# Last residual, final norm and store with tokens on partitions, and two waits taken from the expert passes

## The reference

```python
def _moe(h, w_router, b_router, we1, we3, we2):
    logits = (x @ w_router).astype(f32) + b_router.astype(f32)
    top_v, top_i = lax.top_k(logits, TOP_K)            # 2 of 8 experts for each token
    gates = jax.nn.softmax(top_v, axis=-1)
    comb = jnp.sum(jax.nn.one_hot(top_i, N_EXPERTS, dtype=f32) * gates[..., None], axis=1)
    for e in range(N_EXPERTS):
        y = y + comb[:, e:e + 1] * _swiglu(x, we1[e], we3[e], we2[e]).astype(f32)
...
    x = x + g2 * ffn          # g2: 1024 gates, one row for the prompt, one for each of the 8 sequences
...
    y = _rmsnorm(x, p['final_g'])
```

## Time and profile before

| what | us |
|---|---|
| time, median of 3 runs | 2700.26 |
| lowest and highest of these | 2694.53, 2711.96 |
| time of the profiled execution | 2696.46 |
| its span, first to last instruction | 2694.8 |
| PE busy | 2305.4 (86%) |
| DVE busy | 1541.6 (57%) |
| ACT busy | 1156.8 (43%) |
| POOL busy | 150.9 (6%) |

### The profile page before, as it was taken

One profiled execution on the slowest core, in us unless ns is written; L12 is line 12 of the kernel. 1 busy time (PEld: TensorE's weight loads), 2 busy tenths in 40 slices (PEclk: granted clock), 3 DMA queues, 4 the chain that ended last, 5 costly groups with the idle time before them and its releaser, 6 DMA issues. The chain is left out here.

```text
span 2694.8 us, 37681 instructions
## 1 busy us (share of the span) xinstructions
PE 2305.4 (86%) x14185; PEld 1986.0 (74%) x14185; DVE 1541.6 (57%) x2167; ACT 1156.8 (43%) x1551; POOL 150.9 (6%) x256
## 2 busy tenths in 40 slices
PE   6899985778699999898999768576999999999973
PEld 3799763448699989898997535466878787878762
DVE  0456637323543444444565382437888887888864
ACT  3332114322433333333221144225777777777753
POOL 2000001101000000000000011100000000000001
PEclk6699766858799999997997678687999999999985
DMA  7122415351254454541223235108999999999962
GB/s 237 54 79 63 165 56 174 128 179 56 79 157 132 133 140 133 142 142 32 63 79 102 83 101 194 43 7 313 350 348 364 373 354 351 375 356 358 377 245 86
DMA packets 285562, 485.05 MB, mean 180 GB/s; under 512 B 21614, under 2 KB 216696, under 8 KB 285440
## 3 DMA queue, kind: packets, MB, share of 16 engines
q1 hardware_dynamic: 264816, 416.42, 44.7%
q0 software_dynamic: 20624, 66.91, 7.1%
HBM read 455.79 MB, written 26.97 MB: 179 GB/s over the span
## 5 line engine op out<-in xcount | busy, mean ns | idle before, releaser
L837 PE MATMUL banks<-upper_parts,region_split 128*128 128x320 f32 x1664 | 397.3, 314 | 37.1 <-DVE weights_lower L2081 29.3
L2081 DVE TENSOR_TENSOR expert_lower<-expert_ring,region_split 128x1408 fp32r<-128x1408 f32 (+1 forms) x270 | 387.6, 1467 | 28.1 <-ACT region_split L1567 19.0
L837 PE MATMUL banks<-region_split 128*128 128x320 f32 (+1 forms) x1376 | 378.2, 338 | 28.2 <-DVE region L2081 14.8
L837 PE MATMUL banks<-upper_parts,weights_lower 128*128 128x320 f32 x1248 | 390.1, 313 | 0.0
L1567 ACT ACTIVATE region_split<-expert_ring 128x1408 fp32r<-128x1408 f32 (+1 forms) x270 | 330.5, 1256 | 58.4 <-DMA expert_ring<-in_we 50.5
L837 PEld LDWEIGHTS banks<-upper_parts,region_split 128*128 128x128 f32 x1664 | 290.1, 192 | 38.9 <-DVE weights_lower L2081 35.9
L837 PE MATMUL banks<-region_split,upper_parts 128*128 128x512 f32 (+1 forms) x996 | 300.1, 377 | 1.4 <-DVE upper_parts L2081 1.4
L837 PEld LDWEIGHTS banks<-region_split 128*128 128x128 f32 x1376 | 245.5, 189 | 48.4 <-issue 33.2
L837 PE MATMUL banks<-z_weights_upper,upper_parts 128*128 128x256 f32 (+3 forms) x844 | 262.3, 343 | 14.2 <-DVE region_split L2081 14.2
L837 PE MATMUL banks<-expert_lower,upper_parts 128*128 128x512 f32 x720 | 269.2, 374 | 0.0
L1567 ACT ACTIVATE region_split<-weight_ring 128x2048 fp32r<-128x2048 f32 (+2 forms) x72 | 141.0, 1960 | 253.1 <-PE banks L837 226.0
(11 more groups left out here) (294 smaller groups left out, 3575.3 us busy)
## 6 DMA issues: line engine op xcount, KB each, us to landing
expert_ring<-in_we SPq DMA_DIRECT2D x240, 704.0 KB, 8.0
expert_ring<-in_we SPq DMA_DIRECT2D x165, 512.0 KB, 4.5
weight_ring<-in_w_ada SPq DMA_DIRECT2D x48, 1024.0 KB, 7.4
weight_ring<-in_w SPq DMA_DIRECT2D x88, 512.0 KB, 4.6
weight_ring<-in_w_in SPq DMA_DIRECT2D x24, 1024.0 KB, 5.3
weight_ring<-in_w SPq DMA_DIRECT2D x16, 1408.0 KB, 6.3
weight_ring<-in_w_out SPq DMA_DIRECT2D x8, 1024.0 KB, 8.6
y_rows<-hidden_t POOLq DMA_DIRECT2D x15, 512.0 KB, 7.7
```

Of the source, the lines that this page charges most:

```text
L837: return nc.tensor.matmul(out, lhsT, rhs, start=first, stop=last)
L2081: return v.tensor_tensor(out, x, y, op)
```

## The change

1. **Tail.** `YA` and `YC` have five tiles each, and POOL issues all ten gathers in a row. The rest stays with tokens on partitions: DVE adds the second result, multiplies by the gates and adds the residual, on rows of 1024; ACT squares and sums each row (`accum_out`) and takes the root; DVE takes the reciprocal and multiplies by it and by `final_g`; POOL stores each tile of 512 KB. The transposes, the norm over `XT`, the barriers and the copies into `YO` are gone.
2. **Residual and gate rows.** For that, `XT` is turned block by block in place, and the gates are turned into `GATE_ROWS` (two rows of 1024, for the prompt tiles and for the sample tile, on all partitions). Each is a unit of four 128 x 128 blocks in one bank. Five units of the residual stand in `route1` (`EARLY_ROWS`), five more and four of the gates at the start of `ffn1` (`LATE_ROWS`). `KEPT_BY` says who copies each late unit out. `final_g` is loaded on all partitions into `FINAL_ROW`, an eighth transfer on `router_in`.
3. **Passes.** The wait for `product_made` ahead of `down`, in the loop and behind it, is gone; `turn_product` waits for its own part, and parts 0 and 1 are turned into banks 3 and 4, where before they went into 1 and 2.

```diff
-        YA, YC = r(2, D), r(2, D)
+        YA, YC = r(NT, D), r(NT, D)
...
+        def token_rows(t, half):
+
+            return XT[:, 4 * half:4 * half + 4, tiles(t)]
+
+        EARLY_ROWS = [(t, half) for t in range(NT) for half in range(2)][:5]
+        LATE_ROWS = [(t, half) for t in range(NT) for half in range(2)][5:] + [("gates", i, half) for i in range(2) for half in range(2)]
+        KEPT_BY = ["dve", "dve", "act", "act", "act", "act", "dve", "dve", "dve"]
...
-                         (SNUM[:, :], c["slot_numbers"]), (PFIRST[:, :], c["pass_firsts"]))
+                         (SNUM[:, :], c["slot_numbers"]), (PFIRST[:, :], c["pass_firsts"]),
+                         (FINAL_ROW, a["final_g"].rearrange("(one n) -> one n", one=1).broadcast_to([P, D])))
...
                     for t in range(NT):
-                        if t >= 2:
-                            pool.wait_ge(pair_used, t - 1)
                         for dst, slot in ((YA, SLOT1), (YC, SLOT2)):
                             pool.indirect_dma_start(
-                                dst[:, t % 2, :], None, d["y_rows"],
+                                dst[:, t, :], None, d["y_rows"],
...
             for t in range(NT):
-                for half in range(2):
-                    pool.wait_ge(y_rows_ready, 2 * t + half + 1)
...
+                pool.wait_ge(y_rows_ready, t + 1)
+                load(y_out, (o["y_prompt"][0, tiles(t), :] if t < NTP else o["y_sample"].rearrange("b t d -> (b t) d"), YA[:, t, :]))
...
                     turn_hidden(4)
+                    for u, (t, half) in enumerate(EARLY_ROWS):
+                        b = 4 + (2 * NT + u) % 4
+                        claim(b)
+                        for j in range(4):
+                            ins = tr(PS[:, b, tiles(j)], XT[:, 4 * half + j, tiles(t)])
+                        hand(ins, "act", b)
                     take(one_hots_ready)
...
                         first, end = PARTS[part]
+                        wait(product_made, n.value("product_made") - 2 + part)
                         claim(bank)
...
-                                turn_product(f // 4 - 1, f // 4)
+                                turn_product(f // 4 - 1, 2 + f // 4)
...
+                    for u, unit in enumerate(LATE_ROWS):
+                        b = u % 6
+                        claim(b)
+                        for j in range(4):
+                            if unit[0] == "gates":
...
+                                columns = MOD[:, l, 5 * KD + k, 0:1].broadcast_to([P, P]) if unit[1] == 0 else GATES_SPREAD[:, k, :]
+                                ins = mm(PS[:, b, tiles(j)], columns, ident[:, :], True, True)
+                            else:
+                                ins = tr(PS[:, b, tiles(j)], XT[:, 4 * unit[1] + j, tiles(unit[0])])
+                        holder[b] = hand(ins, KEPT_BY[u], b)
...
-                        wait(product_made, n.value("product_made"))
                         down(True, True)
...
-                    wait(product_made, n.value("product_made"))
                     down(False, True)
...
+                    scale_first(0)
                     for t in range(NT):
+                        if t + 1 < NT:
+                            scale_first(t + 1)
+                        take(tokens_summed)
+                        link(func(YC[:, t, :], YA[:, t, :], ACT.Square, accum_out=SQUARES[:, t:t + 1]))
+                        func(TOKEN_ROOT[:, t:t + 1], SQUARES[:, t:t + 1], ACT.Sqrt, scale=1.0 / D, bias=eps[:, 0:1])\
+                            .then_inc(token_root_ready, 1)
...
+                    copy(GATES_SPREAD.rearrange("p k (b t) -> p k b t", t=TS), along(MOD[:, l, 5 * KD:6 * KD, 1:], 3, TS)).then_inc(gates_spread, 1)
+                    keep(range(2))
                     for _ in range(AHEAD):
                         lower(FE)
+                    keep(range(6, 9))
...
+                    def normalise_rows(t):
+
+                        take(token_root_ready)
+                        link(v.reciprocal(TOKEN_ROOT[:, t:t + 1], TOKEN_ROOT[:, t:t + 1]))
+                        stt(YA[:, t, :], YA[:, t, :], TOKEN_ROOT[:, t:t + 1], FINAL_ROW, ALU.mult, ALU.mult).then_inc(y_rows_ready, 1)
...
+                        link(stt(YA[:, t, :], YC[:, t, :], GB[:, t:t + 1], YA[:, t, :], ALU.mult, ALU.add))
+                        link(tt(YA[:, t, :], YA[:, t, :], GATE_ROWS[:, t // NTP, :], ALU.mult))
+                        by_rows = YA[:, t, :].rearrange("p (k c) -> p k c", c=P)
+                        tt(by_rows, by_rows, XT[:, :, tiles(t)], ALU.add).then_inc(tokens_summed, 1)
+                        if t:
+                            normalise_rows(t - 1)
+                    normalise_rows(NT - 1)
```

More of the change, by code:

```diff
@@ L1322, in _ @@
                 if l % 2:
-                    take(router_in, 112)
+                    take(router_in, 128)
                     claim(0, 1)
@@ L1457, in _ @@
                     for part in range(3):
-                        wait(product_made, n.value("product_made") - 2 + part)
                         turn_product(part, 6 + part % 2)
@@ L1481, in _ @@
                     stage(f"ffn{l}")
-                    for t in range(NT):
-                        take(pair_summed)
-                        for half in range(2):
-                            b = 2 * (t % 2) + half
-                            claim(b)
-                            for k in range(4):
-                                ins = tr(PS[:, b, tiles(k)], YA[:, t % 2, tiles(4 * half + k)])
-                            hand(ins, "dve", b)
-                        pe.drain().then_inc(pair_used, 1)
-                    stage(f"resid{l}")
                     continue
@@ L1543, in _ @@
                 stage(f"ffn{l}")
-                stage(f"resid{l}")
-            norm()
-            stage("norm_final")
-            for t in range(NT):
-                for half in range(2):
-                    b = (2 * t + half) % 8
-                    claim(b)
-                    for k in range(4):
-                        ins = tr(PS[:, b, tiles(k)], HT[:, 4 * half + k, tiles(t)])
-                    hand(ins, "act", b)
-            stage("store")
         @block.scalar
@@ L1903, in _ @@
                     func(E2[:, :], E2[:, :], ACT.Exp).then_inc(pair_exp_ready, 1)
+                    for u, unit in enumerate(EARLY_ROWS):
+                        take(for_act)
+                        drained(copy(kept_rows(unit), PS[:, 4 + (2 * NT + u) % 4, :].rearrange("p (k c) -> p k c", c=P)))
                 stage(f"route{l}")
@@ L1964, in _ @@
                         upper(FE)
+                    for u, unit in enumerate(LATE_ROWS):
+                        if KEPT_BY[u] == "act":
+                            take(for_act)
+                            drained(copy(kept_rows(unit), PS[:, u % 6, :].rearrange("p (k c) -> p k c", c=P)))
                     for half in range(2):
@@ L2033, in _ @@
                 stage(f"ffn{l}")
-                stage(f"resid{l}")
-            root()
-            for k in range(KD):
-                modulate(k, VEC[:, V_FIN + k:V_FIN + k + 1], None)
-            stage("norm_final")
-            for u in range(2 * NT):
-                take(for_act)
-                if u >= 4:
-                    act.wait_ge(y_out[u % 4], 16 * (u // 4))
-                drained(copy(YO[:, u % 4, :], PS[:, u % 8, :]))
-                also(y_rows_ready)
-            stage("store")
         @block.vector
@@ L2771, in _ @@
                 stage(f"ffn{l}")
-                stage(f"resid{l}")
-            norm(along(along(VEC[:, V_FIN:V_FIN + KD], 2, NB), 3, TS), None)
-            stage("norm_final")
-            stage("store")
 _INS = ["x_prompt", "x_sample", "c_prompt", "c_sample", "cache_k", "cache_v", "cache_kidx", "state_C", "state_n",
```

83 lines of the change are left out of this document (34 added, 49 removed).

## The result

| what | before | with the change |
|---|---|---|
| first comparison, median, us | 2706.11 (4 runs) | 2668.09 (4 runs) |
| second comparison, median, us | 2709.97 (11 runs) | 2677.94 (6 runs) |
| profiled execution, us | 2696.46 | 2679.24 |

The ratio is 0.988 (95% interval 0.983 to 0.992) in the first comparison and 0.977 (0.972 to 0.982) in the second. By the medians of all executions the change saves 38 and 32 us, by the means 38 and 39; the forecast was 50. The time of 2668 lies in the range of 2637 to 2671, near its upper end; the 2678 of the second comparison lies above it.

A forecast was written before the change was run, and what follows sets the result against it. PE and transfers both near their limit in the passes, PE setting the pace at the wait; the tail bound by its chain. Gains 32.3 + 14.8 + 3.0 = 50.1 us off 2696.46 gave 2646.4; it said 2648, range 2637 to 2671.

The forecast's parts named there:

- The tail: From first gather to last store: the chain of work tile by tile gets shorter, 32.3 us gained, bounds 29 to 34.5.
- The sum on DVE: In the tail: DVE's operations added up, 3.8 us for a tile's sum and 1.5 for its norm, 5.3 a tile.
- The lead-in: Ahead of the passes: added PE work lies in idle time and later matmuls run faster, 3 us gained for both places.
- The one-hot products: In the lead-in: with PE kept busy ahead of them they may run at 2.4 GHz, 4.46 to 2.4 us.
- The two waits: PE's waits for the product ahead of `down`, in and behind the loop: 14 x 1.06 = 14.8 us gained, bounds 0 to 18.
- At bank 5 it may ... I stay at 14.8: In `up`: the wait on the split product may grow by what was saved; unused transfer time speaks against it, so 14.8 us stays.
- the starving of the earlier trace: Around the wait ahead of `down`: transfers ran at 255 and 183 GB/s, leaving 1.5 us of transfer time unused.
- the 13.1 us: PE's wait on the split product, 11 times in twelve passes, read as `up`'s claim of bank 5 for the third part.
- The first: Rival: the transfers set the pass; PE comes earlier to bank 5 and waits there; 2663 to 2667 us, chance 0.20.
- the transfers' total: In a pass: 18.3 MB at an HBM limit of about 358 GB/s, so the pass couldn't be shorter than it is.
- The rival of the clock: In the passes: a PE without pauses is held back more often, time 2700 or 2717 us; chance 0.02.
- The exchange of banks: In the passes: turning parts 0 and 1 into banks 3 and 4 costs nothing, as DVE reads these long before row 4.

The follow-up runs named there:

- e8: Changed kernel without the multiplication by the gates in the tail; tail 40.0 us, where the change had 45.3.
- e7: Changed kernel without the ten units that turn the residual (four of the gates stay); lead-in 132.23 us, where the change had 128.67.
- e3: Changed kernel with ACT and DVE splitting the turned product ahead of the row of weights behind which it stood; 48.02 us a pass.
- e4: Changed kernel with two matmuls instead of three for each product in the expert passes; 44.70 us a pass.
- e1: Changed kernel with the two waits for the whole product put back ahead of `down`, banks 3 and 4 kept; 50.65 us a pass.
- e2: Changed kernel with product parts 0 and 1 turned into banks 1 and 2 as before, the waits still away; 50.75 us a pass.
- e6: The kernel of e3 with the two waits for the whole product put back ahead of `down`; 49.84 us a pass.
- e11: The kernel of e3, timed against the kernel before; median 2634.69 us, ratio 0.970.
- e12: The changed kernel again, timed beside e11 against the kernel before; median 2677.94 us, ratio 0.977.
- e5: Changed kernel with the `up` rows of weights loaded and split over half their columns, its own order of splits; 47.85 to 47.87 us a pass.

## Why the prediction was right or wrong

- **The tail: right.** 32.3 forecast; 33.5 to 34.0 in the executions with the full tail (45.3 to 45.7 us). The sum on DVE was the right one (e8). A tile took 5.10 us, and not 5.3, since neighbouring operations overlap a little.
- **The lead-in: right.** 3.0 forecast; 3.2 measured, 3.4 in the mean of eleven. The one-hot products went from 4.46 to 2.4 as worked out (in the first changed trace only to 3.94), and e7 shows that it hangs on the added rows.
- **The two waits: wrong.** The step that failed is "At bank 5 it may ... I stay at 14.8": I took the starving of the earlier trace rows as proof that the weights, and with them everything at bank 5, would move along with PE. What moves bank 5's end is ACT's and DVE's order: the last splits of the product stand behind rows of weights that arrive at the transfers' full rate. That chain didn't start earlier: the splits end 0.83 us later behind the turns. The reading of the earlier trace rows was wrong as well: the 13.1 us are waits at bank 2, for part 1, so two parts stood in the way and not one. Without a dip a pass gained 50.53 - 50.21 = 0.3 us instead of 1.06, and the dips took that back: 14.8 forecast, 4 in the first pair of traces, about nothing over the 48 passes (50.81 against 50.75).
- **The rivals.** The first had the place right ("PE comes earlier to bank 5 and waits there"), its time was the nearest (2663 to 2667, chance 0.20), and its sign nearly came: a pass still at 50.5 with 2.2 us at bank 5 was named, and it was 50.41 with 1.74 at banks 4 and 5 together. Its mechanism, the transfers' total, is refuted by e3 and e4. That 2668 lies inside the range owes nothing to the two waits. The rival of the clock had a real effect and the wrong cause: I had a PE without pauses held back, but it was held back behind pauses, at 1.7 us a dip.
- **The exchange of banks** was put at nothing, and no run shows it to cost more. It moved part 1's wait from bank 2 to bank 4. With it and the two waits (e1) a pass took 50.65 us against 50.75 before; without it (e2) 50.75 against 50.81 of the changed code.

The sum after the runs: tail 33.8, lead-in 3.4, twelve passes 0.7 lost, the stretch behind them 1.3 lost in the mean of its four executions, so 35 us, between the 38 and 32 of the two comparisons. That the 14.8 were there to be had is shown by e6 against e3: with the product split first, the two waits are worth 1.8 us a pass, 25.5 us over the twelve passes and the stretch behind them (688.03 against 662.55), of which 6.7 are longer busy time of PE.

What stays open is why e6's wait for the product is 1.06 in some passes and 2.0 in others, and why passes with the same idle time at the banks dip in some cases (28) and not in others (34).

## What to carry to other kernels

When a wait is taken away, follow the engine to its next wait and ask what sets the end of that one. If it is another engine working through a fixed order, the saved time arrives there as longer waiting, unless that order changes too. A low rate of the transfers at the wait says that they could do more, not that the work behind them will come earlier: here a short urgent split (0.5 us) stood behind a long one (1.4 us) that could wait, and exchanging the two gave 2.8 us a pass, 43 in the timed medians (e11 against e12), where removing the wait gave none. And pauses of PE can cost more than their length, when its clock falls behind them.

## What the runs showed of the hardware

The clock fell behind pauses of 1.6 us and more in 28 passes of 62 that had them, and not at all in the 36 of e3, e5 and e11, with 0.6 us at most at a time, so a full PE was the faster and the steadier one (47.86 or 47.87 us in nearly all passes of these three).

POOL's copy of one column, 0.18 us before and in e1 and e6, took 1.05 in the twelve passes of the changed kernel, and up to 1.95 in e3. DVE and POOL in the change, then in e3:

```profile
2089.95 2.35 DVE L2081 TENSOR_TENSOR expert_lower<-expert_ring,region_split 128x1024 fp32r<-128x1024 f32 x2
2091.30 1.05 POOL L768 COPY pass_tokens<-token_table 128x1 int32 x1 [29.97 <-PE banks L848]
```

```profile
2067.74 2.35 DVE L2081 TENSOR_TENSOR expert_lower<-expert_ring,region_split 128x1024 fp32r<-128x1024 f32 x2
2068.19 1.95 POOL L768 COPY pass_tokens<-token_table 128x1 int32 x1 [28.35 <-PE banks L848]
```

The copy ends when DVE's subtraction with two operands in SBUF ends: 2092.35 and 2092.30, 2070.14 and 2070.09. In the trace of before DVE was idle at the copy. The issue of the gather behind it grew in the same way, from 1.08 to 1.85 us and up to 4.1 in e3. The Trainium skill (SBUF — State Buffer, Who interferes with whom) says that DVE and GpSimd share a port pair under an exclusive lock, and that a DVE instruction with two SBUF inputs contends with a GpSimd instruction that reads SBUF; the rows agree. It cost nothing here, since the gathered tokens are needed some 35 us later, and e3, with the longest copies, is the fastest of the kernels that leave nothing out.
